# Residual in column layout, norms by a matmul with ones, and the down projection after all gate/up products, summed in PSUM

## Chip, cores and metric

One core of one Trainium2 chip. The metric is the device time of one execution of the kernel in microseconds; the kernel before takes 1344.52 us, the median of three runs (1343.32 to 1344.72).

## What is computed

One layer of a hybrid decoder over 1024 new prompt rows and 8 decode rows, 1032 rows in all, D_MODEL = 1024, all in float32. The inputs are the rows and the weights; the outputs are the layer's rows, the last keys and values, and the recurrent states.

```python
def _rmsnorm(x, g):
    y = xf * lax.rsqrt(jnp.mean(xf * xf, axis=-1, keepdims=True) + EPS)
    return (y * g.astype(F32)).astype(x.dtype)

h = _rmsnorm(x, g_pre_mix)
aq, ak, av, rq, rf, ri, rg = jnp.split(h @ w_in, SPLIT_POINTS, axis=-1)
...          # window attention with sinks; HGRN2 recurrence with per-head norm and gate
mix = jnp.concatenate([a, o], axis=-1).astype(x.dtype) @ w_out
x = x + _rmsnorm(mix, g_post_mix)
h2 = _rmsnorm(x, g_pre_ffn)
ffn = (jax.nn.silu(h2 @ w_gate) * (h2 @ w_up)) @ w_down      # D_FF = 2816
x = x + _rmsnorm(ffn, g_post_ffn)
```

## The kernel before

Every engine has its own program, written out by hand; semaphores tie them together, and the SyncE program (SP) issues all DMAs in its order. Activations of the projections lie in column layout, [128 features, 8 feature tiles, 1032 rows]: `act_hi` and `act_lo`. To keep float32 accuracy on the fast float32r path, each operand is split into a high part (a rounding copy on ACT) and a low part (a subtraction). A product of 128 output features for one of three chunks of 344 rows is 8 x 3 = 24 matmuls: weight high with activation high and low, weight low with activation high. `products` (L1013) issues them. The weight tile's high part is written by ACT (`weight_hi`, through `copy`, L702), its low part by POOL (`weight_lo`, L616); `raw` holds two incoming tiles, `w_hi`/`w_lo` four split ones.

Head and main stage: 22 input tiles x 3 chunks are 66 units u, each two ticks. The first 12 units are ordered chunk by chunk over the four tiles LEAD, so that PE can start when the first rows are normed. The norm goes by row tiles of 128 rows (`NORM_ROWS`): ACT squares the rows with a sum along them, takes the root, DVE takes the reciprocal of 128x1 and scales (L1337), PE turns the rows to columns by eight transposes (`rows_to_cols`, L1003), ACT and DVE split them from PSUM (L702, L1345). Attention and recurrence run tick by tick between the halves of the units.

Middle stage: 36 slots. Slots 0 to 23 are the output projection, 8 tiles x 3 chunks, the last chunk first; ACT evicts into `mix`. Slots 24 to 35 are gate and up of the first group. Between products, for each of nine row tiles: PE turns `mix` to rows (`cols_to_rows`, L1230), ACT squares and sums, DVE scales (L1637), POOL or DVE adds x (L450), SP stores x2 to a DRAM scratch, ACT and DVE norm again (L1645), PE turns back (L1003), ACT and DVE split.

FFN: 11 groups of two 128-wide tiles of D_FF. Per group `up` is 12 products (288 matmuls) and `down` 144 matmuls (L1295): each of 24 accumulations takes 6 matmuls in one of four banks, and DVE adds the bank to `mix` (L1683, the first group copies, L1681). Groups 1 to 9 are a hardware loop on each engine. The hidden tile goes DVE `hf` (L1627), ACT `h_hi`, POOL `h_lo` (L650); w_down goes ACT `d_hi`, POOL `d_lo` (L655). The last group's chunks are 344, 344, 208 and 136 columns wide, and in it `last_rows` turns finished rows (L1230), ACT squares them, DVE scales (L1659), POOL or DVE adds x2 (L696, L1665), SP stores.

## Time and profile before

| | us |
|---|---|
| median of three runs (lowest, highest) | 1344.52 (1343.32, 1344.72) |
| the profiled execution: its own time | 1345.39 |
| its span in the profile | 1343.6 |
| mean granted TensorE clock | 0.993 |

The page's second part cuts the span in 40 slices of 33.6 us; each digit is the busy share in tenths (9: 90% or more), PEclk is the granted TensorE clock in tenths:

```profile
PE   6999999999999999999999999999999999999997
DVE  5776466655557613353131212121222222222216
ACT  6554434423121524562212121211111121212104
POOL 4021111111232312425323223232323131313115
PEclk9999999999899999999999999999999999999999
DMA  7221100012022332433020302020203030302024
```

The first slice holds the head, slices 2 to 14 the main stage, slices 15 to 18 the middle stage, and the rest the FFN, where a group takes two slices. Of the groups of instructions the page gives, these are the largest of each engine (busy us, mean ns of one | idle before it, and what ended that):

```profile
L1013 PE MATMUL pair<-act_hi,w_hi 128*128 128x344 f32 x1680 | 547.9, 326 | 3.0 <-DVE mix L1431 2.6
...
L616 POOL TENSOR_TENSOR w_lo<-raw,w_hi 128x1024 fp32r<-128x1024 f32 x70 | 167.2, 2400 | 288.7 <-ACT w_hi L702 288.4
...
L1295 PE MATMUL pair<-h_hi,d_hi 128*128 128x344 f32 (+2 forms) x544 | 173.8, 319 | 0.2 <-POOL d_lo L655 0.2
...
L1683 DVE TENSOR_TENSOR mix<-mix,pair 128x344 f32<-128x344 f32 (+2 forms) x248 | 123.9, 501 | 104.7 <-PE pair L1295 104.6
...
L702 ACT ACTIVATE w_hi<-raw 128x1024 fp32r<-128x1024 f32 x70 | 71.5, 1047 | 9.6 <-DMA raw<-w_gate_dram 5.4
```

A matmul's own duration (326 ns) is longer than the distance between two of them, since they are pipelined; distances are read from the chain of waits.

### The profile page before, as it was taken

The numbers are of one execution on the slowest core, as the hardware profiler recorded it, in microseconds if no ns is written. First come the engines' busy times: TensorE is split into PE (matmuls) and PEld (weight loads), VectorE is DVE, ScalarE is ACT, GpSimd is POOL, SyncE is SP. The second block draws the span as 40 slices with busy tenths as digits, with TensorE's granted clock in tenths as the row PEclk, the third lists the DMA queues.
The fourth block names the chain that finished last, engine by engine and source line by source line (L and its number), as shares of the span: only waits on it lengthen the run. The fifth ranks groups of instructions, "written<-read, shape, count | busy, mean of one in ns | idle before, by whom it ended". The sixth has DMA issues, their size and how long they took to land.

```text
span 1343.6 us, 21767 instructions
## 1 busy us (share of the span) xinstructions
PE 1311.6 (98%) x8700; PEld 1290.2 (96%) x8700; DVE 519.9 (39%) x1121; ACT 386.2 (29%) x856; POOL 357.3 (27%) x217
## 2 busy tenths in 40 slices
PE   6999999999999999999999999999999999999997
PEld 6989999999988999999999999999999999999997
DVE  5776466655557613353131212121222222222216
ACT  6554434423121524562212121211111121212104
POOL 4021111111232312425323223232323131313115
PEclk9999999999899999999999999999999999999999
DMA  7221100012022332433020302020203030302024
GB/s 235 54 81 34 32 17 25 26 32 66 17 81 74 87 96 80 147 105 95 1 94 0 94 0 94 0 94 0 94 0 94 0 94 0 94 0 78 1 83 171
DMA packets 105085, 82.83 MB, mean 62 GB/s; under 512 B 13176, under 2 KB 96136, under 8 KB 105008
## 3 DMA queue, kind: packets, MB, share of 16 engines
q1 hardware_dynamic: 105024, 81.99, 19.7%
q8 instruction: 42, 0.69, 0.2%
q14 instruction: 19, 0.16, 0.0%
HBM read 71.02 MB, written 11.99 MB: 62 GB/s over the span
## 4 chain that ended last, share of the span: by engine, by line
PE 65%; DVE 2%; ACT 2%; issue 0%; POOL 0%; ACTq 0%
PE pair L1013 43%; PE pair L1295 19%; PE pair L1230 1%; DVE mix L1431 1%; PE pair L1139 0%; PE pair L1003 0%; ACT L726 0%; DVE x2r L450 0%; PE pair L1212 0%; DVE tr L1637 0%; ACT tr L929 0%; PE pair L1218 0%; ACT tr L924 0%; DVE act_lo L1451 0%; DVE ty L1659 0%
## 5 line engine op out<-in xcount | busy, mean ns | idle before, releaser
L1013 PE MATMUL pair<-act_hi,w_hi 128*128 128x344 f32 x1680 | 547.9, 326 | 3.0 <-DVE mix L1431 2.6
L1013 PE MATMUL pair<-act_hi,w_lo 128*128 128x344 f32 x1680 | 538.0, 320 | 0.0
L1013 PE MATMUL pair<-act_lo,w_hi 128*128 128x344 f32 x1680 | 537.6, 320 | 0.0
L1013 PEld LDWEIGHTS pair<-act_hi,w_hi 128*128 128x128 f32 x1680 | 317.3, 189 | 8.7 <-issue 2.9
L1013 PEld LDWEIGHTS pair<-act_lo,w_hi 128*128 128x128 f32 x1680 | 317.0, 189 | 0.8
L1013 PEld LDWEIGHTS pair<-act_hi,w_lo 128*128 128x128 f32 x1680 | 316.9, 189 | 0.0
L616 POOL TENSOR_TENSOR w_lo<-raw,w_hi 128x1024 fp32r<-128x1024 f32 x70 | 167.2, 2400 | 288.7 <-ACT w_hi L702 288.4
L1627 DVE TENSOR_TENSOR hf<-pair,sg 128x344 f32<-128x344 f32 x66 | 34.1, 516 | 436.2 <-PE pair L1013 436.2
L1295 PE MATMUL pair<-h_hi,d_hi 128*128 128x344 f32 (+2 forms) x544 | 173.8, 319 | 0.2 <-POOL d_lo L655 0.2
L1295 PE MATMUL pair<-h_hi,d_lo 128*128 128x344 f32 (+2 forms) x544 | 173.3, 319 | 0.0
L1295 PE MATMUL pair<-h_lo,d_hi 128*128 128x344 f32 (+2 forms) x544 | 172.1, 316 | 0.0
L1683 DVE TENSOR_TENSOR mix<-mix,pair 128x344 f32<-128x344 f32 (+2 forms) x248 | 123.9, 501 | 104.7 <-PE pair L1295 104.6
L650 POOL TENSOR_TENSOR h_lo<-hf,h_hi 128x344 fp32r<-128x344 f32 x66 | 61.6, 933 | 347.1 <-ACT h_hi L702 347.1
L702 ACT ACTIVATE h_hi<-hf 128x344 fp32r<-128x344 f32 x66 | 32.4, 492 | 246.1 <-DVE hf L1627 246.1
L1295 PEld LDWEIGHTS pair<-h_hi,d_lo 128*128 128x128 f32 x544 | 102.7, 189 | 0.0
L1295 PEld LDWEIGHTS pair<-h_hi,d_hi 128*128 128x128 f32 x544 | 102.2, 188 | 0.5 <-POOL d_lo L655 0.5
L1295 PEld LDWEIGHTS pair<-h_lo,d_hi 128*128 128x128 f32 x544 | 102.2, 188 | 0.0
L655 POOL TENSOR_TENSOR d_lo<-draw,d_hi 128x1024 fp32r<-128x1024 f32 x22 | 52.5, 2407 | 164.5 <-ACT d_hi L702 164.5
L702 ACT ACTIVATE d_hi<-draw 128x1024 fp32r<-128x1024 f32 x22 | 22.2, 1053 | 189.9 <-PE pair L1295 189.9
L702 ACT ACTIVATE w_hi<-raw 128x1024 fp32r<-128x1024 f32 x70 | 71.5, 1047 | 9.6 <-DMA raw<-w_gate_dram 5.4
L911 ACT ACTIVATE sg<-pair 128x344 f32<-128x344 f32 x66 | 30.3, 459 | 141.8 <-PE pair L1013 141.7
L1139 PEld LDWEIGHTS pair<-hq,hk 128*127 128x127 f32 (+6 forms) x448 | 48.3, 182 | 5.2 <-DVE hk L1444 3.6
(215 smaller groups left out, 1313.6 us busy)
## 6 DMA issues: line engine op xcount, KB each, us to landing
raw<-w_gate_dram SPq DMA_DIRECT2D x22, 512.0 KB, 3.8
raw<-w_up_dram SPq DMA_DIRECT2D x22, 512.0 KB, 4.2
draw<-w_down_dram SPq DMA_DIRECT2D x22, 512.0 KB, 5.0
raw<-w_in_dram SPq DMA_DIRECT2D x18, 512.0 KB, 4.7
xr<-x_prompt_dram SPq DMA_DIRECT2D x14, 512.0 KB, 5.2
x_scratch<-x2r SPq DMA_DIRECT2D x8, 512.0 KB, 5.3
x2b<-x_scratch SPq DMA_DIRECT2D x2, 2048.0 KB, 7.9
y_prompt_out<-x2b SPq DMA_DIRECT2D x8, 512.0 KB
```

The costliest lines, as they stand in the source:

```text
L616: pool.tensor_tensor(lo, raw[:, (n if slot is None else slot) % 2], hi.bitcast(F32), ALU.subtract)\
L650: pool.tensor_tensor(h_lo[:, j, cols(c)], hf[:, e, :], h_hi[:, j, cols(c)].bitcast(F32), ALU.subtract)\
L655: pool.tensor_tensor(d_lo[:, j, :], draw[:, j, :], d_hi[:, j, :].bitcast(F32), ALU.subtract)\
L702: return act.activation(out, in_, ACT.Copy)
L911: act.activation(sg[:, e, :], bank[e][:, 0:CW], ACT.Silu).then_inc(sem("gate_done"), 1)
L1013: mm = pe.matmul(out, a[:, k, :], b[:, k, cols(c)], start=(k == 0 and s == 0), stop=(k == KT - 1 and s == 2))
L1139: mm = pe.matmul(BL[n % 2][0:P - hs, P // 2 * c:P // 2 * (c + 1)], hk[:, P * c:P * c + P - hs], qv[:, c, :, 1, :], start=True, stop=True)
L1230: mm = pe.transpose(out[0:w, m // 4, P * (m % 4):P * (m % 4) + P], mix[:, m, r:r + w], ident[:])
L1295: mm = pe.matmul(bank[4 + v % 4][:, 0:cw], a[:, j, P * m:P * m + P], b[:, j, c0:c0 + cw], start=(j == 0 and s == 0), stop=(j == 1 and s == 2))
L1431: dve.tensor_tensor(dst, dst, th[:, s % 2, 0:w], ALU.mult).then_inc(sem("th_read"), 1)
L1627: dve.tensor_tensor(hf[:, e, :], bank[2 + e][:, 0:CW], sg[:, e, :], ALU.mult).then_inc(sem("hf_done"), 1)
L1683: dve.tensor_tensor(acc, acc, src, ALU.add).then_inc(sem("acc_done"), 1)
```

## The change

Layout: `packed` on the host hands x over in column layout, chunk by chunk (`x_cols`), and the gains as columns; the output `y_cols` is in columns too and turned back on the host. All 36 sets of transposes between rows and columns go.

Norms: the squares of the eight feature tiles are summed (by DVE, POOL, or in PSUM), and a float32 matmul with a 128x128 tile of ones sums over the partitions and gives every partition the result. Root and reciprocal then run over the columns of a chunk (128x344 or 128x400), and scaling takes eight instructions per chunk. Head: `first_stat`, `first_norm`, `first_high`, `first_low`. Middle stage: `chain_steps` gives the slots, relative to a chunk's first slot: p_root 8, t 9, squares of x2 9 to 11, q_root 12, h2 13 and 14; the statistics matmul stands in the middle of the slot's product. `mix` keeps x2 to the end; the DRAM scratch for it goes.

FFN: gate/up runs over all 11 groups with no down block between; `hf` goes to a DRAM scratch `h_scratch`. Then the down projection runs in 66 steps v: three column chunks `DCH` of 400, 400 and 232 columns times 22 tiles of D_FF, eight PSUM banks holding the sums. Each step loads its w_down tile and its piece of h (three buffers `DR`), ACT splits off both high parts, DVE `d_lo`, POOL `h_lo` (four tiles `DH`). Between chunks DVE evicts the banks (`take_y`), ACT squares, POOL sums, and the last bank is held back for three steps (`HELD`) for the statistic.

The core of the diff:

```diff
+DCH = ((0, 400), (400, 400), (800, 232))
+NDOWN = len(DCH) * FT
+DR, DH = 3, 4
+HELD = 3
+Y_ROOT, Y_T, Y_STORE = 3, 6, 16
+PRE_MIX, POST_MIX, PRE_FFN, POST_FFN = range(4)
...
+        first_root(0)
+        weight_hi(0)
+        first_high(0)
+        weight_hi(1)
+        first_squares(1)
+        weight_hi(2)
 
...
+            if tick == 4:
+                first_root(1)
+                first_squares(2)
+                weight_hi(3)
+                first_high(1)
+            if tick == 12:
+                first_root(2)
+                first_high(2)
...
+        def first_low(c):
+            for k in range(1, KT, 2):
+                pool.wait_ge(sem("n_hi"), KT * c + k + 1)
+                pool.tensor_tensor(act_lo[:, k, cols(c)], x_tile(k, c), act_hi[:, k, cols(c)].bitcast(F32), ALU.subtract)\
+                    .then_inc(sem("n_lo_p"), 1)
+        weight_lo(0)
+        first_low(0)
+        for n in range(1, LEAD):
             weight_lo(n)
+        first_low(1)
+        first_low(2)
         pool.wait_ge(sem("const_in"), NCONST)
...
+        def first_norm(c):
+            dve.wait_ge(sem("n_std"), c + 1)
+            then(dve.reciprocal(inv0[:], sum0[:]))
+            if c == 0:
                 dve.wait_ge(sem("g_in"), 16)
+            for k in range(KT):
+                x = x_tile(k, c)
+                dve.scalar_tensor_tensor(out=x, in0=x, scalar=gain[:, PRE_MIX, k:k + 1], in1=inv0[:], op0=ALU.mult, op1=ALU.mult)\
+                    .then_inc(sem("n_h"), 1)
+                for j in (k - 1,) if k % 2 else ():
+                    dve.wait_ge(sem("n_hi"), KT * c + j + 1)
+                    dve.tensor_tensor(act_lo[:, j, cols(c)], x_tile(j, c), act_hi[:, j, cols(c)].bitcast(F32), ALU.subtract)\
+                        .then_inc(sem("n_lo_v"), 1)
...
+    def chain_steps(slot):
+
+        out = []
+        for i in range(CH):
+            r = slot - NOUT * i
+            out += [(name, i) for name, at_slot in (("p_root", 8), ("t", 9), ("x2_a", 9), ("x2_b", 10), ("x2_c", 11), ("q_root", 12),
+                                                    ("h_a", 13), ("h_b", 14)) if r == at_slot]
+        return out
...
+                if step == "t":
+                    pool.wait_ge(sem("xc_in"), 16 * (i + 1))
+                    for k in range(KT):
+                        pool.wait_ge(sem("p_t"), KT * i + k + 1)
+                        x = mix[:, k, cols(BACK[i])]
+                        pool.tensor_tensor(x, x, xc[:, k, :], ALU.add).then_inc(sem("x2"), 1)
...
+                        dve.wait_ge(sem("mix_ev"), NOUT * i + k + 1)
+                        dve.scalar_tensor_tensor(out=x, in0=x, scalar=gain[:, POST_MIX, k:k + 1], in1=pinv[:], op0=ALU.mult, op1=ALU.mult)\
+                            .then_inc(sem("p_t"), 1)
...
+            products(out, w, c, 0, 4)
+            for step, i in stats:
+                if step == "p_root":
+                    stat(bank[6][:, 0:CW], psum_[:], "p_sum", (NOUT - 1) * (i + 1), "p_stat")
+                else:
+                    stat(bank[7][:, 0:CW], qsum[:], "q_sum", (KT - 1) * (i + 1), "q_stat")
...
+        def x2_sum(i, ks):
+            for k in ks:
+                dve.wait_ge(sem("q_sq"), KT * i + k + 1)
+                v = (KT - 1) * i + k - 1
+                if v:
+                    dve.wait_ge(sem("q_sum"), v)
+                dve.tensor_tensor(qsum[:], qsum[:], sqq[:, k % 2, :], ALU.add).then_inc(sem("q_sum"), 1)
...
+        def h2_rows(i, ks):
+            for k in ks:
+                v = KT * i + k
+                if v >= 4:
+                    dve.wait_ge(sem(("h2_lo_v", "h2_lo_p")[k % 2]), (v - 4) // 2 + 1)
+                dve.scalar_tensor_tensor(out=hr[:, k % 4, :], in0=mix[:, k, cols(BACK[i])], scalar=gain[:, PRE_FFN, k:k + 1], in1=qinv[:],
+                                         op0=ALU.mult, op1=ALU.mult).then_inc(sem("h2_f"), 1)
+                if k % 2:
+                    h2_low(i, k - 1)
...
+        def down(v, m):
+            i, f = divmod(v, FT)
+            cw = DCH[i][1]
+            (hi, lo), h = d_tiles[v % DH], slice(P * m, P * m + P)
+            if f == 0 and i:
+                pe.wait_ge(sem("y_ev"), KT * (i - 1) + m + 1)
+            for s, (a, b) in enumerate(((hi, h_hi), (hi, h_lo), (lo, h_hi))):
+                mm = pe.matmul(acc(m)[:, 0:cw], a[:, h], b[:, v % DH, 0:cw], start=(f == 0 and s == 0), stop=(f == FT - 1 and s == 2))
+            if f == FT - 1:
+                mm.then_inc(sem("acc_mm"), 1)
+            elif m == KT - 1:
+                mm.then_inc(sem("down_mm"), 1)
+
+        for v in range(NDOWN):
+            i, f = divmod(v, FT)
+            pe.wait_ge(sem("d_split"), v + 1)
+            pe.wait_ge(sem("h_split"), v + 1)
+            held = i > 0 and f < HELD
+            if i and f == HELD - 1:
+                cw = DCH[i - 1][1]
+                pe.wait_ge(sem("y_sum"), (KT - 1) * i)
+                pe.wait_ge(sem("y_ev"), KT * i)
+                pe.matmul(acc(KT - 1)[:, 0:cw], ones[:], ysum[:, 0:cw], start=True, stop=True).then_inc(sem("y_stat"), 1)
+            for m in range(KT - 1 if held else KT):
+                if v == 0 and m == 4:
+                    pe.wait_ge(sem("gate_done"), 6 * GROUPS)
+                    pe.wait_ge(sem("hf_done"), 6 * GROUPS)
+                down(v, m)
+            if held and f == HELD - 1:
+                pe.wait_ge(sem("y_std"), i)
+                for late in range(HELD):
+                    down(v - f + late, KT - 1)
...
+        def load_down(v):
+            i, f = divmod(v, FT)
+            c0, cw = DCH[i]
+            if v >= DR:
+                sp.wait_ge(sem("d_split"), v - DR + 1)
+            elif v == 0:
+                sp.wait_ge(sem("h2_lo_v"), 4 * CH)
+                sp.wait_ge(sem("h2_lo_p"), 4 * CH)
+            sp.dma_start(draw[:, v % DR, :], t_in["w_down"][0, P * f:P * f + P, :]).then_inc(sem(f"draw_in{v % DR}"), 16)
+            if v >= DR:
+                sp.wait_ge(sem("h_split"), v - DR + 1)
+            if i == 0:
+                sp.wait_ge(sem(f"h_out{f % 2}"), 16 * (f // 2 + 1))
+            sp.dma_start(hraw[:, v % DR, 0:cw], h_d[f][:, c0:c0 + cw]).then_inc(sem(f"hraw_in{v % DR}"), 16)
...
+        take_y(last)
+        dve.wait_ge(sem("y_std"), last + 1)
+        then(dve.reciprocal(yinv[:, 0:cw], ystd[:, 0:cw]))
+        for k in range(KT):
+            scale_y(last, k)
+            if k % 2:
+                x = yo[:, k - 1, c0:c0 + cw]
+                dve.wait_ge(sem("y_t"), KT * last + k)
+                dve.tensor_tensor(x, x, mix[:, k - 1, c0:c0 + cw], ALU.add).then_inc(sem("y_done_v"), 1)
```

## Rows read from the trace of the kernel before

**Rows 1.** The page, part 1: engine, busy us (share), instructions.

```profile
PE 1311.6 (98%) x8700; PEld 1290.2 (96%) x8700; DVE 519.9 (39%) x1121; ACT 386.2 (29%) x856; POOL 357.3 (27%) x217
```

**Rows 2.** Chain of waits in order of time, 600 to 720: start, length, what.

```profile
620.28 23.07 PE pair L1295 x144
...
643.35 45.27 PE pair L1013 x288
...
688.62 22.81 PE pair L1295 x144
```

**Rows 3.** The same chain, 1300 to the end of the span.

```profile
1301.27 9.51 PE pair L1295 x60
...
1322.61 2.00 PE pair L1295 x18
...
1328.35 2.63 PE pair L1295 x24
...
1333.18 0.02 issue
...
1339.07 2.07 DVE x2b L1665
```

**Rows 4.** Table of waits, PE: who waited <- for whom: us in total, times, longest.

```profile
PE pair L1003 <- DVE hr0b L1337: 2.7, 2, 1.7
...
PE pair L1003 <- DVE tr L1645: 0.7, 1, 0.7
```

**Rows 5.** Chain of waits, 424 to 436 us, an f32 matmul of 512 columns.

```profile
431.24 1.91 PE pair L1212 x4
```

**Rows 6.** Chain of waits, 500 to 650 us, sets of eight transposes.

```profile
509.86 0.87 PE pair L1230 x8
...
514.50 0.59 PE pair L1003 x8
```

**Rows 7.** Timeline of DVE and POOL: start, length, instruction, idle before.

```profile
229.59 2.40 POOL L616 TENSOR_TENSOR w_lo<-raw,w_hi 128x1024 fp32r<-128x1024 f32 x1 [19.87 <-ACT w_hi L702]
...
230.87 0.29 DVE L1496 TENSOR_TENSOR orow<-pair,rden 128x128 f32<-128x128 f32 x1
...
248.93 1.04 POOL L638 TENSOR_TENSOR hg<-r_f 128x512 f32<-128x512 f32 x1 [16.94 <-DVE f_s L1411]
...
254.46 2.37 POOL L616 TENSOR_TENSOR w_lo<-raw,w_hi 128x1024 fp32r<-128x1024 f32 x1 [0.86 <-ACT w_hi L702]
...
254.61 2.37 DVE L1474 TENSOR_TENSOR q_lo<-mix,q_hi 128x128 fp32r<-128x128 f32 x1 [0.71 <-ACT q_hi L702]
...
314.80 1.22 DVE L1504 TENSOR_TENSOR hq<-r_q,r_f 128x1024 f32<-128x1024 f32 x1
...
314.84 2.08 POOL L638 TENSOR_TENSOR hg<-r_f 128x512 f32<-128x512 f32 x1 [15.94 <-DVE f_s L1411]
```

**Rows 8.** Groups by form, DVE and POOL: busy us, mean ns | idle before.

```profile
L1382 DVE TENSOR_TENSOR mix<-mix,hk 128x344 f32<-128x344 f32 x12 | 6.2, 517 | 0.4
...
L1491 DVE RECIPROCAL rden<-den 128x2 f32<-128x2 f32 x32 | 5.3, 166 | 1.1
...
L1547 DVE RECIPROCAL orstd<-ostd 128x8 f32<-128x8 f32 x4 | 0.8, 203 | 30.0 <-ACT ostd L726 30.0
...
L650 POOL TENSOR_TENSOR h_lo<-hf,h_hi 128x344 fp32r<-128x344 f32 x66 | 61.6, 933 | 347.1 <-ACT h_hi L702 347.1
```

**Rows 9.** Timeline of PE, 55.9 to 56.8 us.

```profile
56.31 0.32 PE L1013 MATMUL pair<-act_hi,w_hi 128*128 128x344 f32 x1
```

**Rows 10.** Timeline, 7 to 9 us, ACT.

```profile
8.20 1.06 ACT L734 ACTIVATE hr<-xr 128x1024 f32<-128x1024 f32 x1 [2.55 <-DMA xr<-x_prompt_dram]
```

**Rows 11.** Busy time by windows, 1304 to 1305: engines, then PEclk, DMA share, GB/s.

```profile
1304.00:1305.00 1.00, 1.00 (x8) 1.00 (x7) 0.51 (x1) 0.00 (x0) 0.00 (x0) 1.00 1.03 422
```

**Rows 12.** Busy time by windows, 339 to 348 us.

```profile
339.00:348.00 9.00, 8.51 (x36) 8.07 (x35) 6.14 (x10) 0.00 (x0) 2.01 (x1) 0.50 0.01 2
```

**Rows 13.** The tile draw (loads of w_down), its landings.

```profile
DMA to landing us min/median/max: 3.6/5.0/6.8
```

773 lines of the change are left out of this document (373 added, 400 removed).

## The prediction

> **What bounds the kernel now.** I read the page first: PE is busy 98% of the span, and no other engine over 39% [rows 1]. The reader is to see there that only PE's own work, or a new gap in it, can move the time. The chain of waits says the same: from 601 to 1333 us it is one engine, ten down blocks of 22.8 us (the first 23.1) between ten gate/up blocks of 45.3 us, and a last down block with seven sets of eight transposes in it [rows 2, 3]. The table of waits then asks what PE lacked: nothing over 1.7 us at a time after the first load [rows 4]. So three quantities decide: how long PE's instructions are, how many fall away, and whether the new producers (DVE, POOL, ACT) keep up as the old ones did.
>
> Spacings. Gate/up: 45.27/288 = 157 ns for 344 columns. Down: 22.81/144 = 158.4 ns, which is 344/2.4 = 143.3 ns at full clock plus 15.1. Blocks of 208 columns took 2.00/18 = 111 ns and of 136 columns 2.63/24 = 110 ns [rows 3]: about 110 is a floor, and the narrow 232-column chunk lies just above it.
>
> **Down projection.** Before it takes 23.07 + 9 x 22.81 + (1333.18 - 1301.27 = 31.9) = 260.3 us. After: chunks of 400, 400 and 232 columns, 528 matmuls each: 1056 x (400/2.4 + 15.1 = 181.8 ns) = 192.0 us and 528 x (232/2.4 + 15.1 = 111.8 ns) = 59.0 us, together 251.0. Two statistics matmuls of 400 columns come to it. No f32 matmul with ones is in the trace; the nearest row is L1212, f32 with 512 columns, four records for two calls in 1.91 us, so 0.95 us a call [rows 5]: by columns 0.74 us for 400, 0.64 for 344, 0.43 for 232 (bounds: 0.11, what one narrow matmul takes, and 0.95). Sum 252.5, so -7.8 us before stalls. The adds of L1683 on DVE go, but they hid behind PE and free nothing.
>
> **Where the transposes go, in the middle stage.** 18 sets of eight (nine L1230, nine L1003), 17 of 0.87 us and one of 0.59 [rows 6]: 15.4 us off PE, and the wait of 0.7 us before the last L1003 [rows 4]. Six statistics matmuls come: +3.8. Without new stalls -12.3 us. The same edit takes the round trip of x2 through DRAM away; its DMAs lay beside PE and give nothing.
>
> **The cover for this is DVE and POOL, and there I find the price.** Look at both engines together [rows 7]: a q_lo of 128x128 elements on DVE took 2.37 us beside a 2.37 us POOL subtraction and ended with it; a POOL product took 2.08 us beside DVE's 1.22 us hq, its like at 248.93 only 1.04. A DVE read of PSUM keeps its time: L1496 at 230.87, inside the POOL subtraction that began at 229.59, took 0.29 us. So DVE work with two SBUF inputs and POOL work take turns, whole instructions at a time. This is the Trainium skill's rule too (GPSIMD Engine Reference, Key points: contention with VectorE instructions with two SBUF inputs); the trace agrees, and by that rule alone, without durations, no other sum follows. In the kernel before nearly all DVE work of the middle stage reads PSUM or runs alone. In the new one nearly all is SBUF with SBUF.
>
> Prices [rows 8]: DVE 344 columns 0.52 us, POOL 344 columns 0.93, ACT eviction 0.45. The reciprocal now runs over columns: 166 ns for 2, 203 ns for 8, so 6.2 ns an element and 2.3 us for 344 (bounds 0.52, as other DVE work of 344 columns, and 4.6, twice the slope, if it too met POOL).
>
> Middle stage, per chunk, from the start S of the p statistic in slot 8: matmul 0.64, root 0.5, reciprocal 2.3, so S+3.4. Then eight scalings and eight POOL adds in turns, 8 x 1.45 = 11.6; then nine DVE sums still open (seven of q, about two of the next chunk's p) x 0.52 = 4.7: S+19.7. PE comes to the q statistic four slots later, at 0.64 + 4 x 3.77 = S+15.7. Stall 4.0 us. The second chunk has POOL's w_lo of slots 19 and 20 (2.4 us each) in the same turns; half of one counts: 5. For the third the sums of p are gone (-1) and w_lo of slot 24 comes (+1.2): 4.1, and then a table load 1.28, root, reciprocal and 12 x 0.52 + 4 x 0.93 = 9.9 us of h2 in turns, 14.1 us, against 3.5 slots = 13.2: 0.9. Sum 14.0. Queued behind these waits on ACT are the evictions, which have a slot to spare. Middle stage: -12.3 + 14.0 = +1.7.
>
> **Head.** Before, the ninth product (u = 8) starts at 56.31 [rows 9]; eight products are 30.2 us, so this stretch was already set by what feeds PE. After, x of chunk 0 (1.4 MB behind 64 KB; before, 1.6 MB had landed when the second square began at 8.20 [rows 10]) is there at 7.5; squares 0.7, two matmuls, root: 10.2; reciprocal 12.5. POOL is in w_lo(0) until 13.7. Then 12 x 0.52 + 4 x 0.93 = 9.9 us in turns, and PE's k steps follow that supply: unit 0 ends at 24.1. w_lo(1) only now: unit 1 from 26.2 to 30.0. Unit 2 follows the statistic, 30.6 to 34.4. ACT then squares chunk 2 before w_hi(3), POOL ends w_lo(3) at 37.3: unit 3 to 41.1. Chunk 1's norm has DVE and POOL in turns after w_lo(3), 8.9 us more: 46.2, units 4 to 7 to 61.9 with a statistic. Chunk 2's root comes after unit 5, 54.9, reciprocal 57.2, turns 9.9: u = 8 starts at 67.1. Against 56.3: +10.8 us. If the engines did not take turns, the three norms would be 3.7 us shorter each: +1.5 at most, as the other delays stay hidden.
>
> **Moved work with a cover.** Gate/up of group 1 now follows group 0 at once. ACT starts w_hi after silu of gate 5, 0.46 + 1.05 and POOL's 2.40, 4.06 us against one product of 3.77: +0.3. Before, a down block stood there (22.8 us of cover). In the loop the same steps have three products' time and store 1 MB of h a group beside 2 MB of weights; nothing late. The stores of h that are queued on SP ahead of loads wait for hf, at most half a group, and the raw tiles behind them have 22 us.
>
> **Down, the producers.** In a 400-column slot (24 x 181.8 ns = 4.4 us) the turns are DVE 1.22 [rows 7] + POOL 1.08: fine. In a 232-column slot of 2.7 us they are 1.22 + 0.63, plus, over eight slots, a scaling 0.59 and an add 1.08 of the chunk before: 3.5 us. Four tiles of lead hide most; I take 2.0 (bounds 0 and 7). Between chunks the statistic needs seven POOL adds of 1.08 = 7.6 us after the first square; PE passes two slots of 21 matmuls, 7.6 us with 400 columns but 4.7 with 232: stall 2.3 at the last change of chunk. Together 4.3. DMA: 643 KB a slot is 240 GB/s, with the stores of y 270; the x2b load ran at 422 GB/s with all DMA engines busy [rows 11], so it fits, but only three buffers turn over: 4 us to land (draw loads took 3.6 to 6.8 [rows 13]), 1.05, 1.22 and turns, about 7.5 us for three slots of 8.0. Down in all: -7.8 + 4.3 = -3.5.
>
> **Tail.** Before, 1343.6 - 1333.18 = 10.4 us after the last product. After, from its end E: last eviction and square E+1.5, statistic 2.1, root 2.5, reciprocal of 232 4.1, then 12 x 0.39 on DVE and 4 x 0.63 on POOL in turns 7.3: E+11.4, store issue and landing 2.8 (before: 2.4 from the end of the last add, 2.07 us long from 1339.07 [rows 3]): 14.2. So +3.8.
>
> **Sum.** Head +10.8, middle +1.7, group change +0.3, down -3.5, tail +3.8: +13.1 us. On the profiled execution, 1345.4 us (span 1343.6 and 1.8 around it), this is 1358.5; the profiled one lies 0.9 above the median of the three runs, so 1358.
>
> **Rivals.**
> 1. The turns cost little, because the instructions meet less often than I assume. For it: nearly every old DVE row is undisturbed. Against: in each chain both engines have work ready all the time. Head +1.5, middle -12.3, group change +0.3, down -7.8, tail +1.2 (DVE's 4.7 alone): -17.1, so 1327. This is the case on the other side of no change: of the 30 us between it and the forecast, less than 17 may come as stalls if the kernel is to be faster.
> 2. PE's clock falls in the new gaps. At 339 to 348 us the granted clock was 0.50, the 1.2 GHz level, with the 8- and 64-column matmuls of the attention and recurrence in and before that stretch [rows 12]; half of its 9 us was lost. My gaps are of 4 to 5 us: two in the head, up to three in the middle. From nothing to 4.5 us each, five of them give up to +22: 1380 at the end, 1369 in the middle. [...]
> 3. The last chunk starves on its three buffers: a landing of 6.8 us, the slowest of the draw loads, would make 22 slots 0.8 us longer each, +17 on the forecast: 1375.
> 4. It doesn't do what it says: no transposes remain in the text of the change, so none is left on PE. No chance is given to it.
>
> **How the numbers follow.** Forecast 0.44, between 1349 and 1366. Rival 1: 0.29. Rival 2: 0.17. Rival 3: 0.05. A mix of forecast and rival 1 that ends within 0.2% (2.7 us, about what a measurement tells from no change): 0.05. Faster: 0.29 plus a little of the mix, 0.30; same 0.05; slower 0.65. The range, 1325 to 1378, leaves out somewhat under half of rival 1 below and the top of rival 2 above, under 0.2 together. The likeliest case's own is 1349 to 1366.
>
> **What would show it.** In the waits, PE behind DVE's sums in the q statistic by 3 to 6 us three times; u = 8 at 65 to 69 us; DVE instructions with SBUF inputs at twice their length beside POOL; matmuls of 400 columns every 182 ns and of 232 every 112; the end of the span 14 us after the last product. Wrong: if DVE's 344-column instructions stay at 0.52 in the chains and u = 8 starts before 60, rival 1 holds; a granted clock of 0.5 in slots 12 to 28 is rival 2.

## The result, and the profile of the changed kernel

The changed kernel takes 1372.05 us, the median of four runs (1367.22 to 1374.31), beside 1344.61 (1343.32 to 1344.72) for the kernel before: a ratio of 1.0202, 95% interval 1.0173 to 1.0230. It is slower by twice what was forecast (+27.4 us against +13.4). The profiled execution took 1371.6 us with a span of 1369.8 and a mean granted clock of 0.981, so 26.2 us more span than before. One execution of r2 (below) took 6308.66 us and one of the kernel before 1867.23; both are left out of every comparison.

Part 1 and part 2 of the page of the changed kernel, the rows that answer to [rows 1] and to the table of slices ahead:

```profile
PE 1307.3 (95%) x8433; PEld 1278.8 (93%) x8433; DVE 573.5 (42%) x1011; ACT 422.4 (31%) x892; POOL 406.2 (30%) x262
...
PE   7879999999999999989999999999999999999896
...
DVE  5986557573657647872000000000001122463484
...
POOL 4221120112131233453221212122223033564483
PEclk8999999999999999999999999999999999999998
```

PE is still what bounds the kernel, but 95% busy, not 98%. It waits in slices 1 to 3, 18 and 38. In slices 2 and 3 DVE is at 9 and 8 tenths, in 16 to 18 at 7 and 8 (before 3 to 5), and in slice 39 DVE and POOL are both at 8.

The table of PE's waits (line waited for: us in total, times, longest), which answers to [rows 4]:

```profile
PE pair L1047 <- ACT mix L713: 8.9, 2, 7.5
PE pair L1047 <- ACT sqp L976: 7.8, 4, 2.7
...
PE pair L1350 <- POOL h_lo L694: 5.0, 2, 3.8
...
PE pair L1274 <- DVE qsum L1679: 2.3, 1, 2.3
```

Before, the longest was 1.7 us. The rows lie where the norms are: the head (L713), the middle stage (L976, L1679) and the change of chunk in down (L694).

The stages of both profiled executions, from the timeline of PE:

| from, to | before, us | after, us | difference | forecast |
|---|---|---|---|---|
| start to the last wait for `mix` of the recurrence | 471.03 | 488.49 | +17.5 | +10.8 |
| middle stage, with the start of gate/up | 149.25 | 153.02 | +3.8 | +2.0 |
| the other ten groups of gate/up | 452.7 | 452.9 | +0.2 | 0 |
| down | 260.3 | 261.4 | +1.1 | -3.5 |
| tail | 10.4 | 14.0 | +3.6 | +3.8 |

**The head.** DVE and POOL in the changed kernel, the norm of chunk 0, and then DVE ahead of the norm of chunk 2 (start, length, instruction, idle before):

```profile
17.60 1.72 DVE L1392 SCALAR_TENSOR_TENSOR mix<-mix,gain,inv 128x344 f32<-128x344 f32 x2
19.25 0.50 DVE L1396 TENSOR_TENSOR act_lo<-mix,act_hi 128x344 fp32r<-128x344 f32 x1
...
17.70 1.25 POOL L615 TENSOR_TENSOR act_lo<-mix,act_hi 128x344 fp32r<-128x344 f32 x1 [1.46 <-ACT act_hi L713]
...
52.62 6.82 DVE L1383 TENSOR_REDUCE sum<-sq 128x344 f32<-128x2752 f32 x1
...
63.55 2.29 DVE L1387 RECIPROCAL inv<-sum 128x344 f32<-128x344 f32 x1
```

The turns are there as in [rows 7]: the second of each pair of scalings stands still while POOL subtracts, 1.72 us for two that take 1.06 alone (the pairs that start at 38.53 and 65.88 in the same trace). But the reduction over the eight feature tiles takes 6.82 us, and behind it stand two ropes (the rotary embedding of a unit, four DVE instructions of some 0.5 us each), 59.36 to 63.55. The reciprocal of chunk 2 starts at 63.55; the forecast had it at 54.9.

### The profile page after: what moved, and what is told of

The parts are those of the page before. It is cut to its first block, busy times and chain, and to the rows that moved or that the text cites. A ratio compares the mean times of both kernels' runs of the same rounds, so it can differ in the third digit from the quotient of the medians.

```text
span 1369.8 us, 21037 instructions
## 1 busy us (share of the span) xinstructions
PE 1307.3 (95%) x8433; PEld 1278.8 (93%) x8433; DVE 573.5 (42%) x1011; ACT 422.4 (31%) x892; POOL 406.2 (30%) x262
## 4 chain that ended last, share of the span: by engine, by line
PE 57%; DVE 5%; POOL 3%; issue 2%; ACT 1%; POOLq 0%; ACTq 0%; DVEq 0%
PE pair L1047 41%; PE pair L1335 14%; DVE mix L1705 2%; POOL h_lo L694 2%; POOL ysum L702 1%; DVE qsum L1679 1%; DVE mix L1480 1%; POOL yo L686 1%; DVE hr L1691 1%; DVE pinv L1700 1%; PE pair L1184 0%; PE pair L1274 0%; PE pair L1257 0%; DVE psum__128 L1724 0%; PE pair L1263 0%
## 5 line engine op out<-in xcount | busy, mean ns | idle before, releaser
L1335 PE MATMUL pair<-h_hi,d_hi 128*128 128x400 f32 (+1 forms) x528 | 170.9, 324 | 1.1 <-POOL h_lo L694 1.1
L1335 PE MATMUL pair<-h_hi,d_lo 128*128 128x400 f32 (+1 forms) x528 | 170.0, 322 | 0.0
L1335 PE MATMUL pair<-h_lo,d_hi 128*128 128x400 f32 (+1 forms) x528 | 169.6, 321 | 0.0
L694 POOL TENSOR_TENSOR h_lo<-hraw,h_hi 128x400 fp32r<-128x400 f32 (+1 forms) x66 | 101.9, 1547 | 147.0 <-ACT h_hi L713 146.7
L1743 DVE TENSOR_TENSOR d_lo<-draw,d_hi 128x1024 fp32r<-128x1024 f32 x66 | 91.9, 1398 | 127.7 <-ACT d_hi L713 127.6
L713 ACT ACTIVATE d_hi<-draw 128x1024 fp32r<-128x1024 f32 x66 | 70.0, 1060 | 142.1 <-PE pair L1335 101.6
L713 ACT ACTIVATE w_hi<-raw 128x1024 fp32r<-128x1024 f32 x70 | 73.7, 1055 | 52.5 <-PE pair L1047 43.5
L1184 PE MATMUL pair<-hq,hk 128*127 128x64 f32 (+6 forms) x448 | 47.5, 259 | 3.3 <-DVE hk L1493 3.3
L855 ACT ACTIVATE prob<-sm,negm 128x256 f32<-128x256 f32 (+1 forms) x64 | 31.2, 488 | 51.5 <-DVE tsum L1533 51.5
```

The lines of the kernel that those rows point to most:

```text
L694: pool.tensor_tensor(h_lo[:, v % DH, 0:cw], hraw[:, v % DR, 0:cw], h_hi[:, v % DH, 0:cw].bitcast(F32), ALU.subtract)\
L713: return act.activation(out, in_, ACT.Copy)
L855: act.activation(prob[:, e, g, k0:], sm[:, g, k0:], ACT.Exp, bias=negm[:, e, g:g + 1], scale=SCALE, accum_out=den[:, e, g:g + 1])
L1184: mm = pe.matmul(BL[n % 2][0:P - hs, P // 2 * c:P // 2 * (c + 1)], hk[:, P * c:P * c + P - hs], qv[:, c, :, 1, :], start=True, stop=True)
L1335: mm = pe.matmul(acc(m)[:, 0:cw], a[:, h], b[:, v % DH, 0:cw], start=(f == 0 and s == 0), stop=(f == FT - 1 and s == 2))
L1743: dve.tensor_tensor(lo[:], draw[:, v % DR, :], hi[:].bitcast(F32), ALU.subtract)\
```

## Experiments

All ratios are to runs of the kernel before on the same chip. Where the profiled executions are compared, the marks are these starts (us; "main" is the start behind the last wait for `mix` at the end of the main stage, "down" and "last" are the first and last matmul of the down projection; the kernel before has no such mark for "down"):

| kernel | unit 16 | main | down | last | span | median | ratio (95%) |
|---|---|---|---|---|---|---|---|
| before | 105.45 | 471.03 | | 1332.9 | 1343.6 | 1344.61 | |
| changed | 126.41 | 488.49 | 1094.27 | 1355.55 | 1369.8 | 1372.05 | 1.0202 (1.0173 to 1.0230) |
| e1 | 121.90 | 486.14 | 1087.88 | 1348.82 | 1363.1 | 1371.35 | 1.0197 (1.0171 to 1.0223) |
| e2 | 125.76 | 491.01 | 1084.16 | 1346.08 | 1360.3 | 1360.52 | 1.0108 (1.0081 to 1.0135) |
| e3 | 127.21 | 492.47 | 1095.72 | 1348.88 | 1368.0 | 1368.55 | 1.0168 (1.0132 to 1.0205) |
| e4 | 127.81 | 491.66 | 1093.40 | 1350.19 | 1364.4 | 1369.63 | 1.0193 (1.0160 to 1.0225) |
| g1 | 126.86 | 487.36 | 1087.56 | 1352.55 | 1366.8 | 1371.68 | 1.0198 (1.0168 to 1.0228) |
| g2 | 121.71 | 483.83 | 1085.61 | 1348.20 | 1362.5 | 1363.81 | 1.0135 (1.0105 to 1.0165) |
| g3 | 118.70 | 480.80 | 1073.95 | 1330.29 | 1344.5 | 1348.65 | 1.0022 (1.0010 to 1.0034) |
| h2 | | 482.35 | 1075.49 | 1327.92 | 1344.6 | 1346.55 | 1.0003 (0.9989 to 1.0017) |
| h3 | | 482.51 | 1075.68 | 1328.11 | 1344.8 | 1344.96 | 0.9999 (0.9984 to 1.0015) |

Head and main stage are the same code in the changed kernel, e3 and e4, and "main" lies between 488.5 and 492.5: so much do profiled executions differ by themselves.

**e1: the reduction as three adds.**

```diff
-            dve.tensor_reduce(sum0[:], sq0[:].rearrange("p k r -> p r k"), AX.X, ALU.add).then_inc(sem("n_sum"), 1)
+            then(dve.tensor_tensor(sq0[:, 0:4, :], sq0[:, 0:4, :], sq0[:, 4:8, :], ALU.add))
+            then(dve.tensor_tensor(sq0[:, 0:2, :], sq0[:, 0:2, :], sq0[:, 2:4, :], ALU.add))
+            dve.tensor_tensor(sum0[:], sq0[:, 0, :], sq0[:, 1, :], ALU.add).then_inc(sem("n_sum"), 1)
```

> Edit: in the head, the one DVE reduction over eight feature tiles (6.84 and 6.82 us in the trace of the changed kernel) becomes three contiguous adds of 1376, 688 and 344 columns, some 1.6 + 0.8 + 0.5 = 2.9 us. Theory A (the reduction is what the prediction mis-sized, 3 us for 6.8, and everything behind it in DVE's queue waits): PE's unit 2 starts 3 to 4 us earlier, unit 8 at 68 to 70 us instead of 75.8, and the kernel ends 5 to 8 us earlier, 1364 to 1367. Rival B (the head is set by DVE and POOL taking turns in the three norms, the reduction lies in slack): unit 8 moves by less than 2 us and the time stays at 1370 to 1374.

The adds took 1.58, 0.88 and 0.52 us for chunk 2. Unit 8 started at 71.13 instead of 75.80, unit 16 was 4.5 us earlier and the span 6.7 shorter. So rival B's unit 8 is refuted and theory A holds in kind, with less than it asked at unit 2 (33.30 for 34.77). The median moved by 0.7 only, which is inside rival B's band; r1 and r2 below take that up.

**e2: the norms' work of POOL on DVE** (the odd tiles' low parts in the head and of h2, and the adds of x in the middle stage; POOL keeps the weights).

```diff
-                        pool.tensor_tensor(x, x, xc[:, k, :], ALU.add).then_inc(sem("x2"), 1)
...
+                            xj = mix[:, j, cols(BACK[i])]
+                            dve.tensor_tensor(xj, xj, xc[:, j, :], ALU.add).then_inc(sem("x2"), 1)
```

> Edit: the odd low parts of the first norm, the add of x in the middle stage and the odd low parts of h2 move from POOL to DVE; DVE gets 16 more instructions of 0.52 us per chunk in all, POOL loses as many of 0.93 us. Theory A (DVE work with two SBUF inputs and POOL work take turns, so the sum of both counts): each first norm 9.9 to 8.3 us, the scaling and adding of a middle chunk 11.6 to 8.3 us, h2 9.9 to 8.3 us; PE's waits on sqp and qsum in the middle stage, 10 us together, fall under 2 us, the granted clock there goes back to 1.0, and the kernel ends 10 to 18 us earlier, 1354 to 1362. Rival B (the two engines work side by side, and the chains are long because DVE is): DVE has more to do, each chain becomes 2 to 4 us longer, the waits grow, the time is 1376 to 1390.

11.5 us faster than the changed kernel although DVE has more to do: theory A. The timeline of a norm in the middle stage, first the changed kernel (DVE, POOL, ACT, PE), then e2 (DVE, ACT, PE):

```profile
520.56 8.03 DVE L1705 SCALAR_TENSOR_TENSOR mix<-mix,gain,pinv 128x344 f32<-128x344 f32 x8
528.51 1.24 DVE L1724 TENSOR_TENSOR psum__128<-psum__128,sqp 128x344 f32<-128x344 f32 x1
...
521.28 9.25 POOL L662 TENSOR_TENSOR mix<-mix,xc 128x344 f32<-128x344 f32 x8 [16.96 <-DVE mix L1705]
...
531.00 1.74 ACT L940 ACTIVATE sqq<-mix 128x344 f32<-128x344 f32 x3 [5.75 <-DVE qsum L1679]
...
533.48 0.65 PE L1047 MATMUL pair<-act_hi,wx_hi 128*128 128x344 f32 x1 [2.70 <-ACT sqp L976]
```

```profile
524.49 0.57 DVE L1691 SCALAR_TENSOR_TENSOR mix<-mix,gain,pinv 128x344 f32<-128x344 f32 x1
524.98 0.51 DVE L1698 TENSOR_TENSOR mix<-mix,xc 128x344 f32<-128x344 f32 x1
525.40 0.57 DVE L1691 SCALAR_TENSOR_TENSOR mix<-mix,gain,pinv 128x344 f32<-128x344 f32 x1
...
531.43 1.73 ACT L926 ACTIVATE sqq<-mix 128x344 f32<-128x344 f32 x3 [3.68 <-DVE qsum L1665]
...
533.91 0.42 PE L1033 MATMUL pair<-act_hi,wx_hi 128*128 128x344 f32 x1 [0.60 <-ACT sqp L962]
```

Eight scalings take 8.03 us beside POOL's eight adds, which take 9.25 from the first to the last: 1.16 us a tile where two engines share, 0.91 (524.49 to 525.40) where DVE does both alone. So spreading this work over two engines costs more than leaving it on one. It costs less than the forecast's full turn of 0.52 + 0.93 = 1.45, though; POOL's add alone is 0.93, so the turns themselves are worth some 0.2 us a tile. The way to PE is by the queues: PE waits for an eviction (ACT's copy out of PSUM), which stands on ACT behind the square of the fourth tile of x2; that square waits for a buffer that DVE's first sum of the squares frees, and this sum stands on DVE behind the eight scalings. From the first scaling to that square it is 10.4 us in the changed kernel and 8.4 in e2, 2.1 less, as PE's wait of 2.70 became 0.60. PE's waits in the middle stage fell from 10.0 us (2.70, 2.71, 0.52, 1.86, 2.26) to 3.3 (0.60, 0.60, 1.31, 0.79), and the stretches at the low clock behind them went: together 12.9 us, and "main" to "down" is 12.6 us shorter (593.2 against 605.8; against the nine profiled executions under g5 below 8.6 to 12.6). In the head it gained nothing. The Trainium skill (SBUF — State Buffer, Who interferes with whom) has the rule for it: a VectorE instruction with two SBUF inputs contends with a GpSimd instruction that reads SBUF. The traces agree: the scalings from the third on take 1.24 us each beside POOL's adds and 0.57 in e2.

**e3: three chunks of 344 columns in down.**

```diff
-DCH = ((0, 400), (400, 400), (800, 232))
+DCH = ((0, 344), (344, 344), (688, 344))
```

> Edit: the down projection's column chunks are 344, 344, 344 instead of 400, 400, 232. PE's own work stays, 1584 x 158.4 ns = 250.9 us against 251.0. Theory A (the down part loses 10 us because in a 232-column slot of 2.7 us DVE and POOL have more than that to do in turns): the waits on h_lo, now 6.1 us, fall under 2 us, the last product ends 8 to 10 us after 1094 + 251 instead of 10.4 us after it, i.e. 5 to 8 us earlier; the tail grows from 14.0 to 17 us with the wider last chunk; net 2 to 5 us earlier, 1367 to 1370. Rival B (the waits come from the three load buffers and DMA): a slot that is 1.1 us longer gives them the same relief at the end, but the stall at the change of chunk (4.0 us for the statistic) stays.

Down from first to last matmul took 253.2 us instead of 261.3, with two waits of 1.7 and none after; the tail took 18.8 instead of 14.0. The median is 3.5 lower, with intervals that overlap. By the traces it is theory A: the 232-column steps were starved, and the wider last chunk takes most of it back at the end. Slower loads would be relieved by a longer step too; the full queues shown further on, in the item on down, speak against them.

**e4: sums and last adds of down on DVE.** `ysum` and `add_x2` move from POOL to DVE.

```diff
-                    pool.tensor_tensor(ysum[:, 0:a], ysq[:, 0, 0:a] if m == 1 else ysum[:, 0:a], ysq[:, m, 0:a], ALU.add)\
+                    dve.tensor_tensor(ysum[:, 0:a], ysq[:, 0, 0:a] if m == 1 else ysum[:, 0:a], ysq[:, m, 0:a], ALU.add)\
```

> Edit: in the down part, POOL's sums of the squares and its adds of x2 between the chunks move to DVE; the adds of the very last chunk stay. Theory A (turns): POOL's seven sums, 1.06 to 1.86 us each, become 0.6 us each on DVE and end right behind the squares, so the waits of the statistic (1.2 and 3.8 us) go; later turns per 232-column slot fall from 1.22 + 0.63 + 0.6 + 1.08 to 1.22 + 0.63 + 0.6 + 0.6 us; the kernel ends 5 to 8 us earlier. Rival B (DVE is the late engine of the down part, d_lo stands behind the sums in its queue): PE waits on d_lo instead, and the time stays within 2 us or grows.

Down 256.8 us, 4.5 less; 2.4 in the median, with intervals that overlap. The rows of the changed kernel and of e4 at the second change of chunk show it (POOL and PE of the changed kernel, DVE and PE of e4):

```profile
1287.70 8.56 POOL L702 TENSOR_TENSOR ysum<-ysum,ysq 128x400 f32<-128x400 f32 x6
1296.23 1.30 POOL L694 TENSOR_TENSOR h_lo<-hraw,h_hi 128x232 fp32r<-128x232 f32 x2
...
1297.00 0.72 PE L1350 MATMUL pair<-ysum,ones 128*128 128x400 f32 x1 [3.78 <-POOL h_lo L694]
```

```profile
1287.67 4.75 DVE L1761 TENSOR_TENSOR ysum<-ysum,ysq 128x400 f32<-128x400 f32 x6
1292.34 2.35 DVE L1733 TENSOR_TENSOR d_lo<-draw,d_hi 128x1024 fp32r<-128x1024 f32 x2
...
1293.61 0.94 PE L1340 MATMUL pair<-ysum,ones 128*128 128x400 f32 x2 [2.46 <-DVE d_lo L1733]
```

PE waited 3.78 us, in the end for `h_lo`, which stood on POOL behind six sums of 1.43 us; the sum itself was done at 1296.26, only 0.7 us before PE went on. Alone on DVE a sum takes 0.79. The first wait (1.21) is gone in e4, but of the second 2.46 us stay, now behind `d_lo` in DVE's queue, which is what rival B named: each theory has a part, and the 5 to 8 us of theory A did not come.

**g1: transposes of the identity in PE's gaps**, so that PE is busy while it waits.

```diff
-        keep_warm(24)
+        keep_warm(48)
...
+                keep_warm({1: 12, 2: 8, 3: 22, 4: 16, 6: 10, 8: 56}.get(u, 0))
...
+                keep_warm({12: 24, 20: 24, 23: 4}.get(slot, 0), BO)
```

> The changed kernel, with transposes of the identity (0.11 us each) set into TensorE's idle gaps, on a PSUM bank that nobody reads: 48 in place of 24 ahead of unit 0, 4 ahead of each k step of unit 0, then 12, 8, 22, 16, 10, 56 ahead of units 1, 2, 3, 4, 6, 8; in the middle stage 24, 24, 4, 16, 18 ahead of slots 12, 20, 23, 24 and the q statistic of slot 28; in down 30 ahead of the second statistic. Nothing else moves. In the profile of the changed kernel the granted clock was 0.50 in ten stretches of 3.3 or 6.7 us, nearly all of them right behind such gaps; busy time in them, halved, comes to 18.8 us, against 6.6 us in the kernel before. Theory A, the gaps cost clock: the stretches behind them go, 6.1 us in the middle, 1.7 in down, some 3 to 5 of the 9.3 in the head (the rest lay in unit 0, which its supply paces), the stretch of the recurrence stays: 1358 to 1363. Theory B, the clock has nothing to do with the gaps, or what it cost was covered by the wait for the next norm: 1369 to 1375, with the same stretches.

Busy time by windows (us, PE, PEld, DVE, ACT, POOL, then the granted clock, DMA share, GB/s), the changed kernel and then g1:

```profile
71.00:79.00 8.00, 3.21 (x12) 3.22 (x13) 6.36 (x15) 5.21 (x10) 2.87 (x3) 0.57 0.00 0
...
532.00:540.00 8.00, 6.52 (x22) 6.05 (x23) 4.02 (x8) 3.29 (x9) 0.00 (x0) 0.57 0.40 161
```

```profile
71.00:79.00 8.00, 6.67 (x54) 6.17 (x52) 6.39 (x12) 5.21 (x10) 3.13 (x4) 1.00 0.00 0
...
532.00:540.00 8.00, 7.92 (x50) 7.49 (x49) 6.34 (x10) 4.03 (x10) 0.00 (x0) 1.00 0.31 125
```

At 570 to 574 and 590 to 595 us, behind the waits of 2.71 and 1.86, the changed kernel has 0.57 and 0.66, g1 1.00 and 1.00. In g1's trace the clock stays up behind every gap that was filled, and its two low stretches before the last product (at 51.59 and 1290.63) lie at waits of 2.51 and 3.79 us that stayed; so in those places the gaps are what lets it fall. What that is worth differs by stage. In the middle "main" to "down" fell by 5.6 us (600.2). In the head unit 8 started at 76.19 against 75.80, no gain at all: there the norms are late whatever PE's speed. In down the 30 transposes came behind the wait for `h_lo`, not into it, and cost 3.7. The median stayed (0.4 less): theory B's time, though theory A's stretches went.

**g2: units 4 and 8 by k steps, and e1's adds.** PE takes each k step of a chunk's first unit as its low part comes; ScalarE's high parts stand behind the evictions.

```diff
-                if 0 < u < LEAD * CH and u % LEAD == 0:
-                    pe.wait_ge(sem("n_lo_v"), 4 * (c + 1))
-                    pe.wait_ge(sem("n_lo_p"), 4 * (c + 1))
...
-            mm = products(J[u % 2][:, 0:CW], w_tiles(n), c, 4 * half, 4 * half + 4, u == 0)
+            mm = products(J[u % 2][:, 0:CW], w_tiles(n), c, 4 * half, 4 * half + 4, u in (0, LEAD, 2 * LEAD))
```

> Head alone: the adds for the reduction as in e1; units 4 and 8 take each k step as its high and low part come, as unit 0 does, where they waited for all eight; for that ScalarE's eight high copies of chunks 1 and 2 stand two ticks later, behind the evictions of units 2 and 6; its high part of weight tile 3 comes ahead of the squares of chunk 2, and VectorE's sum of chunk 2 right behind the norm of chunk 1. In e1 unit 3 started at 40.3, unit 4 at 48.6, unit 8 at 71.1, unit 9 at 77.3 us. Theory A, what the head lost beside the reduction is that PE does not overlap a norm with its chunk's first unit: unit 3 at 38, unit 9 at 66 to 69, so 8 to 11 us less than e1's 1371.35: 1360 to 1364. Theory B, the norm's own chain sets the end of the chunk and the overlap only turns waiting ahead of a unit into waiting within it: 0 to 4 us less, 1367 to 1372.

Unit 8 started at 64.2 instead of e1's 71.1, but unit 9 at 76.9, as in e1 (77.3): PE now waited 6.1 us for the attention's first `q_lo`, which stands behind the norm of chunk 2 on DVE. In the traces nothing is gained at unit 16 (121.71 against 121.90): by its marks this is theory B, with the wait turned into one at the attention. The median, on another chip, is 7.5 lower than e1's, with the intervals apart (1.0105 to 1.0165 against 1.0171 to 1.0223), which is theory A's number. The marks don't show where that comes from; e1's profiled execution was its fastest, 6.5 us under its median, and three of g2's four had a granted clock of 0.986 to 0.987, e1's 0.977 to 0.983.

**g3: e1, e2, e4 and g2 together.**

> e1, e2, e4 and the head of g2 together: the reduction as adds, all of the norms' low parts and the adds of x on VectorE, the sums and the add of x2 of the down projection on VectorE, units 4 and 8 by k steps. Alone these gave 0.7 (in the profiled executions 6.7), 11.5, 2.4 (in the profiled executions 5.4) and, by theory A of g2, 8 to 11. Theory A, each takes away a wait of its own stretch, and they add up: 1372 - 5 - 11.5 - 4 - 9 = 1342 to 1349, so the changed order of work is as good as the old one when its waits are gone. Theory B, the engine that takes them all, VectorE, becomes what the head waits for, and less than half of the head's and down's gains is left: 1351 to 1358.

1348.65 us, 0.2% over the kernel before in place of 2.0%: nearly all of the loss is gone, and theory A holds for the sum. Middle stage and gate/up take 593.2 us as in e2, down 256.3 as in e4. The wait for the first `q_lo` stays, at 5.3 us.

**h1, h2, h3, h4, h6: what is left in the head and in down.** h1 moves the first query block's split ahead of the norm of chunk 2.

```diff
-                if 0 <= i < NITEM:
+                if (step == "Q") <= i < NITEM:
...
+        if tick == 11:
+            out.append(("Q", 0))
```

> g3 with one step moved: the split of the first query block (ScalarE's q_hi, VectorE's q_lo) stands at tick 11, ahead of the norm of chunk 2, where g3 has it at tick 15, behind that norm. In g3 PE waited 5.3 us for that q_lo at 69.6 us, and the granted clock was 0.50 from 67 to 75 us right behind it, which took another 2.3 us. Theory A, the wait and the stretch at the low clock both go: 5 to 7 us less than g3, 1341 to 1344 (g3: 1348.65, kernel before on the same chip 1346.1). Theory B, VectorE's score step of that block comes behind the norm too, and the wait only moves to it: 0 to 2 us less, 1346 to 1349.

h1 took 1348.97 us, 1.0030 (1.0014 to 1.0045): theory B. h2 makes the chunks of down 400, 344 and 288 columns wide, h3 adds short runs of transposes in the middle stage.

> h1 with the down projection's chunks 400, 344 and 288 columns wide instead of 400, 400 and 232. In g3 down took 256.5 us against 252.5 without stalls, and 14.0 from the last product to the end; with three chunks of 344 (e3) down had 1.7 us of waits twice and the tail took 18.8, so 0.043 us a column: 16.4 with 288. Theory A, the supply of a 232-column step (VectorE and POOL in turns) is what is late, and 24 x 135 ns = 3.2 us a step covers it: stalls 0 to 1 instead of 4, tail +2.4, in all 1 to 2 us less than h1. Theory B, the stalls stay and the tail is longer: 1 to 3 us more than h1.

> h2 with short runs of identity transposes in the middle stage's gaps: 5, 5, 11 and 6 of them (0.11 us each) ahead of slots 12, 20, 24 and the q statistic of slot 28, where e2 and g3 waited 0.6, 0.6, 1.3 and 0.8 us. Theory A, in part of the executions of g3 (1350 to 1351 us at a mean granted clock of 0.985 against 1346 to 1348 at 0.991) one of these gaps brings a stretch at the low clock, and this takes it away: median 0.5 to 2 us under h2, with less spread. Theory B, the low stretches lie in the head, the recurrence and the end, as in g3's profile: the same as h2 within 0.5 us.

h2: down 252.4 us and tail 16.4, together 1.5 less than g3's 256.3 and 14.0; the median is 2.4 under h1's: theory A. h3: the stages as in h2; its median is 1.6 lower, within the intervals, so between its theories nothing is decided. h4 moves the whole attention back by one unit, h6 puts DVE's score step ahead of a rope and of the lower bound.

> h3 with the attention's ticks moved back by two (one unit); the recurrence, the decode rows' attention and the lower bound stay where they are. In h1 to h3 PE stood 4.0 us at 72.6 us for the first block's softmax: VectorE's score step came at 70.7, behind the norm of chunk 2, a rope and the lower bound; the granted clock was 0.50 behind it, another 1.4 to 2.4 us. Theory A, with one more unit of products ahead of it the wait goes, and the stretch with it: 4 to 6 us less than h3's 1344.96, 1339 to 1341. Theory B, the later attention meets the recurrence and the decode rows further on, and PE waits there instead: 0 to 2 us less, or slower than h3.

> h3 with VectorE's queue behind the norm of chunk 2 reordered: the lower bound's first half stands at tick 10, ahead of that norm, its second half and the rope of unit 6 behind the score step of the first block. In h3 the score step came at 70.7 to 72 us, 4.8 behind the end of the norm (k_lo 1.0, rope 2.0, lower bound 1.7), and PE waited 4.0 us for the softmax that follows it; h4, which moved the attention instead, kept a wait of 3.0 and got new stretches at the low clock. Theory A, the wait is the queue of VectorE alone: it goes, with 1 to 2 us of low clock behind it: 1339 to 1341 beside the kernel before at 1345. Theory B, the 3.7 us only come later, as waits for the rope or the second block: the same as h3, 1344 to 1346.

h4 took 1347.81 us (1.0014, 1.0002 to 1.0026), h6 1346.05 (1.0006, 0.9990 to 1.0023). The one long wait of PE behind the norm of chunk 2 in g3, h3 and h6 (in h4 it is 3.03, at 79.89):

```profile
69.64 0.55 PE L1106 MATMUL pair<-k_hi,q_hi 128*128 128x256 f32 x1 [5.30 <-DVE q_lo L1497]
```

```profile
74.30 0.47 PE L1116 MATMUL pair<-ident,prob 128*128 128x128 f32 x1 [3.96 <-ACT esk L837]
```

```profile
73.80 0.77 PE L1109 MATMUL pair<-k_hi,q_hi 128*128 128x512 f32 x1 [3.99 <-issue]
```

It moves from one operation to the next and keeps 3 to 5 us, and theory B of h1, h4 and h6 held each time: DVE works from 56 to 74 us with hardly a gap (h3 and h6), so what is put ahead makes something else late. Less work for DVE there should help; that was not tried.

**p1 and p2: the price of a sum.** More reductions on DVE at the end of the changed kernel, with POOL done (their time comes on top of the kernel's).

> The changed kernel with seven more instructions on VectorE after its last add, while POOL is done: the sum over eight tiles of 128x344 as one reduction with the eight terms 400 elements apart; the same with the terms side by side; four terms 400 apart; 128x8 sums over 344 elements in a row; then the three adds of 1376, 688 and 344 elements. The extra time after the end is of no interest, only the lengths. In the profile of the changed kernel the reduction of eight terms took 6.8 us, 2.5 ns an element, and the adds of e1 took 1.59, 0.88 and 0.52. Theory A, the price is that of the stride: the second and fourth reductions take 2.9 us (1.05 ns an element), the first 6.8. Theory B, it is a price for each element or each output of any reduction: the second takes 6.8 too, the third half of it; whether the fourth does decides between element and output. Theory C, it was POOL's work beside it: the first takes 2.9 here.

> The changed kernel with five reductions on VectorE after its last add, each over terms that lie apart: 8 terms 400 elements apart (344 outputs), 8 terms 344 apart, 8 terms 384 apart, 4 terms 344 apart, 8 terms 16 apart (16 outputs). In p1 the first took 4.77 us, 1.73 ns an element, and with the terms side by side 3.02; in the changed kernel's head the same reduction with 344 between the terms took 6.84 and 6.82. Theory A, it is the distance 344: the second takes 6.8 here, too. Theory B, it was what ran beside it in the head (DMA into SBUF, ScalarE): the second takes 4.8 here.

DVE in p1, then in p2 (the five of p2 in one row of 19.31, whose second and third start at 1372.87 and 1379.69):

```profile
1367.60 4.77 DVE L1787 TENSOR_REDUCE ysum<-ysq 128x344 f32<-128x2752 f32 x1 [0.64 <-POOL yo L686]
1372.41 3.02 DVE L1788 TENSOR_REDUCE ysum<-ysq 128x344 f32<-128x2752 f32 x1
```

```profile
1372.87 6.79 DVE L1790 TENSOR_REDUCE ysum<-ysq 128x344 f32<-128x2752 f32 x1
...
1379.69 4.77 DVE L1790 TENSOR_REDUCE ysum<-ysq 128x344 f32<-128x2752 f32 x1
```

With the terms side by side 3.02 us (1.10 ns an element), 400 or 384 apart 4.77 (1.73), 344 apart 6.79 (2.47), with nothing beside it. So the head's 6.8 is how the terms lie, not what ran beside them: p1's theory A is right in kind, p2's theory A in full. (In the head POOL's 2.38 us of `w_lo` lay inside the first reduction and nothing of POOL in the second, with 6.84 and 6.82.) The distance alone does not set the price either: with four terms instead of eight, 344 apart (p2) and 400 apart (p1) both took 2.48 us (1.80 ns an element). The Trainium skill (SBUF — State Buffer, Door 1: The DMA port swizzle) says of SBUF that each access in another 16-byte line pays; the traces agree that far, but all of 344, 384 and 400 leave the line at each step, and no run here shows why eight terms 344 apart cost most.

**r1, r2, g5: are the terms in the median?** The changed kernel, e1 and a g1 with transposes in the middle stage alone, side by side on one chip.

> The changed kernel itself, for comparison with the next two on one chip. 1368 to 1374 us, as before.

> e1 once more (three adds for the reduction). In e1's profile unit 8 started 4.7 us earlier than in the changed kernel's and the span was 6.7 shorter, but its median was only 0.7 lower, on another chip. Theory A, the head's gain reaches the end and the spread of single executions hid it: 4 to 6 us under r1. Theory B, it is made up later, as the attention behind the head is fixed to other work: 0 to 2 us under r1.

> The changed kernel with g1's identity transposes in the middle stage alone (24, 24, 4, 16, 18 of them ahead of slots 12, 20, 23, 24 and the q statistic of slot 28). In g1's profile the middle stage and gate/up took 600.2 us instead of 605.8 and held no stretch at the low clock; the head gained nothing and the transposes ahead of the last statistic lost 3.7. Theory A, the low clock behind the middle stage's stalls costs 4 to 6 us in each execution: that much under r1. Theory B, it costs less in most executions than in the profiled one: 0 to 2 us.

| | unit 16 | main | down | span | median | ratio (95%) |
|---|---|---|---|---|---|---|
| r1, the changed kernel | 128.01 | 492.19 | 1096.77 | 1372.6 | 1372.42 | 1.0190 (1.0167 to 1.0213) |
| r2, adds | 122.58 | 488.30 | 1091.62 | 1366.7 | 1370.37 | 1.0180 (1.0156 to 1.0204) |
| g5, middle kept busy | 126.97 | 493.74 | 1093.97 | 1369.6 | 1369.49 | 1.0172 (1.0150 to 1.0194) |

r2 has the 5.4 us at unit 16 again and a span 5.9 shorter, and again a median that is only 2.1 lower. Two of its executions had a mean granted clock of 0.977, as two of e1's (0.977, 0.978); none of the changed kernel's was under 0.981. A mean lower by 0.004 is 11 us more at half speed in 1370 us, so up to 5.5 us of lost work (an estimate). So part of the gain is lost in some executions to more time at the low clock; why the shorter head brings that was not found.

g5 has no low stretch in its middle stage, "main" to "down" 600.2 against r1's 604.6; its median is 2.9 us lower, with intervals that overlap. The profiled executions settle the term better than the medians. Nine have the same code between those marks (the changed kernel, e1, e3, e4, g2, p1, p2, r1, r2): with one stretch of 3.4 us at a clock of 0.50 they took 601.7 to 601.8 us, with two 603.2 to 603.3, with three 604.6, and with two of 3.4 and one of 6.8 us 605.8. g1 and g5 took 600.2 with none. So each 3.4 us at the low clock cost some 1.5, and the term is 1.5 to 5.6 us, by how many fall in an execution.

## Why the prediction was wrong in size

The direction held, and so did the terms of the group change, gate/up and the tail. The steps in the order of the forecast:

- **Turns of DVE and POOL**: right, and the main thing. e2 takes them away in the middle stage and the kernel is 11.5 us faster. Their price was too high: 1.45 us a tile of scaling and adding in the forecast, 1.16 in the trace. Rival 1 (1327) is refuted by the same run.
- **Head, +10.8 forecast, +17.5 measured (+19.5 at unit 8).** The norms themselves took 8 to 10 us and the reciprocal 2.30, as forecast. The step that failed is the sum over the eight tiles of chunks 1 and 2. The forecast names it nowhere; between the end of the squares (27.42 in the trace) and its statistic (30.0) its times leave under 3 us for it, less than the 3.02 of 2752 elements side by side. It took 6.84 and 6.82, and e1 took 4.7 us off unit 8 by that step alone. The second omission is of the same kind: two ropes (4.2 us) stand between that sum and the reciprocal of chunk 2 on DVE, and "chunk 2's root comes after unit 5" looked at PE's and ACT's order only. This second part is read from the trace; no run took the ropes out. Unit 2 was 4.2 us later than forecast, unit 8 8.7. Of the 19.5 some 2 came back in the main stage, where this execution lost 1.7 us to the low clock and the one of before 6.6 ([rows 12] is the larger part of that).
- **Middle stage, +2.0 with the group change, +3.8 measured.** Without stalls 149.25 - 12.3 = 137.0; measured stalls 10.0 and low clock 6.1 (half of PE's busy time in the stretches at 0.5) give 153.1, and 153.0 was measured. So -12.3 for the transposes fits, 14.0 of stalls was 10.0, and their place was wrong in two of three: PE waited 2.70 and 2.71 for evictions that stood on ACT behind squares, and these waited for DVE's sums behind the scalings (5.75 us at 531.00, under e2). "Which have a slot to spare" was the failing clause. The missing term is the clock. That the total came within 1.8 us is luck: stalls 4.0 too high against a clock of 6.1 left out.
- **Rival 2, the clock**: true as a mechanism, but no rival; it adds to the forecast. Low stretches came to 18.8 us of lost PE time in the changed kernel against 6.6 before. The 9.3 of them in the head cost nothing (g1), those in the middle 1.5 to 5.6 (the nine executions under g5). It should have stood in the sum. The stretch that it was read from (339 to 348 us, [rows 12]) did not bear on gaps: from 325 us to its start PE had no gap over 0.37 us.
- **Group change +0.3**: 0.29 us of wait, right in size, though the forecast's terms (0.46, 1.05, 2.40) add up to 3.91 and not 4.06. **Gate/up**: 452.9 against 452.7, right.
- **Down, -3.5 forecast, +1.1 measured.** A 400-column matmul came every 181.8 ns (92.15/507), as forecast. Marked stalls were 6.0 (1.21, 3.78, 0.69, 0.36) against 4.3, and 1.7 went to the low clock behind the longest. The first statistic took 0.91, near its upper bound. The seven sums were costed alone, 7.6 us; in turns with `d_lo` they took 9.7, and `h_lo` stood behind them. Rival 3, slow landings, was not what starved the last chunk: in 1311 to 1335 us the queues of DVE and POOL were full,

```profile
1314.81 2.06 DVE L1743 TENSOR_TENSOR d_lo<-draw,d_hi 128x1024 fp32r<-128x1024 f32 x1
1316.79 1.06 DVE L1755 SCALAR_TENSOR_TENSOR yo<-yo,gain,yinv 128x400 f32<-128x400 f32 x1
...
1314.40 1.38 POOL L686 TENSOR_TENSOR yo<-yo,mix 128x400 f32<-128x400 f32 x1
1315.74 1.68 POOL L694 TENSOR_TENSOR h_lo<-hraw,h_hi 128x232 fp32r<-128x232 f32 x1
```

  in a period of 2.96 us where PE's step is 2.7. The forecast had 3.5 us for it and let four tiles of lead hide most; the lead did hide most.
- **Tail +3.8**: 14.0 against 14.2, right. In the chain of waits, where [rows 3] has the transposes of before, the statistic starts at 1355.83 and takes 3.15 us with its waits, the root 0.46 and the reciprocal 1.61.

Sum of the misses: head 6.7, middle 1.8, down 4.6, gate/up 0.2, tail -0.2: 13.1, the whole difference between 26.2 and 13.1. The range held because it reached up to rival 2; the forecast's own range, to 1366, did not.

What stays open: why r2 and e1 gain 5 us and more in the profile and 1 to 2 in the median, why g2 gains in the median and not at unit 16, and why eight terms 344 apart cost more than eight 400 apart. The best of the versions, h3, is level with the kernel before (0.9999, 0.9984 to 1.0015); none beat it.

## What to carry to other kernels

When work moves from row layout to column layout, cost each new instruction by its operands: where they lie (here DVE work with two SBUF inputs took turns with POOL, 1.16 us a tile for the pair) and how the terms of a sum lie. The chain whose steps alternated between DVE and POOL was faster on DVE alone. New gaps on PE can cost more than themselves, so put what the clock may take behind them into the sum; and behind each long chain on a queue, list what else stands there before you say what waits.

## What the runs showed of the hardware

- A DVE reduction of 2752 float32 elements took 3.02 us with its terms side by side, 4.77 with them 384 or 400 elements apart, 6.79 with 344; of 1376 elements (four terms) 2.48 with 400 and with 344 between them; the three adds that do the same as the first took 1.59, 0.88 and 0.52.
- A DVE scaling of 128x344 took 0.57 us and a POOL add 0.93 alone; in a chain that alternates between them each tile took 1.16, and 0.91 with both on DVE.
- In the nine profiled executions with the changed kernel's middle stage, PE's waits of 1.85 to 2.71 us for an eviction had a granted clock of 0.50 (the 1.2 GHz level) from about their end on in 18 of 27 cases, for 3.4 or 6.8 us; the nine waits of 2.26 us for the q statistic in none. Behind the waits of 0.6 to 1.3 us in e2, g3, h1 and h2 there was no such stretch. With transposes in the gaps (g1, g5) the clock stayed at 1.00.
- The DVE reciprocal took 2.30 us for 344 columns and 1.61 for 232.
